# A chunked RWKV-7 scan with one transition matrix per chunk, made before the scan

## The reference

```
def step(state, inp):
    r_t, w_t, k_t, v_t, kk_t, a_t = inp
    sa = einsum('bhvk,bhk->bhv', state, -kk_t)
    state = (state * w_t[:, :, None, :] + sa[..., None] * (kk_t * a_t)[:, :, None, :]
             + v_t[..., None] * k_t[:, :, None, :])
    return state, einsum('bhvk,bhk->bhv', state, r_t)
```

## Time and profile before

| what | value |
|---|---|
| median of 3 runs | 2389.5 us (2381.62 to 2393.41) |
| the profiled execution, its own time | 2394.83 us |
| its span | 2392.7 us |
| TensorE busy | 2250.3 us, 94% |
| VectorE, ScalarE, GpSimd busy | 52%, 39%, 31% |
| TensorE's granted clock, mean | 0.977 |

### The profile page before, as it was taken

One profiled execution on the slowest core, in us unless ns is written; L12 is line 12 of the kernel. 1 busy time (PEld: TensorE's weight loads), 2 busy tenths in 40 slices (PEclk: granted clock), 3 DMA queues, 4 the chain that ended last, 5 costly groups with the idle time before them and its releaser, 6 DMA issues.

```text
span 2392.7 us, 46390 instructions
## 1 busy us (share of the span) xinstructions
PE 2250.3 (94%) x19640; PEld 1712.6 (72%) x19640; DVE 1246.5 (52%) x2035; ACT 943.4 (39%) x1681; POOL 735.8 (31%) x384
## 2 busy tenths in 40 slices
PE   8999989999979998988888889999998999999998
PEld 6885778888867647777777777777887666754476
DVE  5028254023155666767777534794213999736123
ACT  4238444233234433444444443554323222343133
POOL 2310334444414203111111033444431433430246
PEclk9999999999979998999999999999997999999999
DMA  4312123233212210000000122343231333222232
GB/s 143 111 60 78 62 72 96 88 101 93 88 42 80 88 44 9 10 10 10 10 10 10 39 71 79 117 179 124 82 106 71 106 117 114 89 87 78 71 94 82
DMA packets 49882, 180.64 MB, mean 75 GB/s; under 512 B 5600, under 2 KB 5856, under 8 KB 49440
## 3 DMA queue, kind: packets, MB, share of 16 engines
q1 hardware_dynamic: 46064, 166.82, 21.6%
q10 hardware_dynamic: 3632, 11.08, 1.2%
HBM read 167.33 MB, written 10.55 MB: 74 GB/s over the span
## 4 chain that ended last, share of the span: by engine, by line
PE 72%; issue 12%; DVE 5%; ACT 5%; POOL 4%; DMA 0%; POOLq 0%; ACTq 0%; DVEq 0%; SPq 0%
PE ps L603 15%; PE ps L604 15%; PE ps L605 15%; PE ps L606 6%; POOL ring_lo L2266 4%; PE ps L904 2%; PE ps L865 2%; PE ps L651 2%; PE ps L895 1%; PE ps L1101 1%; PE ps L722 1%; PE ps L737 1%; PE ps L712 1%; PE ps L1122 1%; PE ps L813 1%
## 5 line engine op out<-in xcount | busy, mean ns | idle before, releaser
L2266 POOL TENSOR_TENSOR ring_lo<-ring,ring_hi 128x1024 fp32r<-128x1024 f32 x240 | 589.8, 2465 | 1019.1 <-ACT ring_hi L1158 1019.0
L605 PE MATMUL ps<-u_lo,ring_hi 128*128 128x512 f32 x968 | 384.8, 398 | 0.0
L1158 ACT ACTIVATE ring_hi<-ring 128x1024 fp32r<-128x1024 f32 x240 | 251.4, 1052 | 105.4 <-DMA ring<-in_wall 102.0
L603 PE MATMUL ps<-mlp_u_hi,ring_hi 128*128 128x512 f32 x512 | 204.6, 400 | 13.6 <-DVE u_lo L1744 9.0
L606 PE MATMUL ps<-arena,ring 128*128 128x512 f32 x480 | 210.5, 594 | 6.0 <-ACT arena L1627 3.3
L605 PEld LDWEIGHTS ps<-u_lo,ring_hi 128*128 128x128 f32 x968 | 183.9, 190 | 43.5
L603 PE MATMUL ps<-mid_hi,ring_hi 128*128 128x512 f32 x512 | 203.3, 397 | 2.6 <-POOL ring_lo L2266 2.6
L604 PE MATMUL ps<-mlp_u_hi,ring_lo 128*128 128x512 f32 x512 | 203.2, 397 | 0.0
L605 PE MATMUL ps<-mid_lo,ring_hi 128*128 128x512 f32 x512 | 202.5, 396 | 0.0
L604 PE MATMUL ps<-mid_hi,ring_lo 128*128 128x512 f32 x512 | 202.5, 395 | 0.0
L603 PE MATMUL ps<-in_u_hi,ring_hi 128*128 128x512 f32 x480 | 193.8, 404 | 5.8 <-POOL gs_lo L2354 2.8
(11 more groups left out here) (434 smaller groups left out, 4335.6 us busy)
## 6 DMA issues: line engine op xcount, KB each, us to landing
ring<-in_wall SPq DMA_DIRECT2D x273, 512.0 KB, 3.7
s_tables<-arena ACTq DMA_DIRECT2D x16, 512.0 KB, 2.7
arena<-s_tables SPq DMA_DIRECT2D x16, 512.0 KB, 3.7
arena<-bias_lines SPq DMA_DIRECT2D x16, 448.0 KB, 4.3
arena<-in_lora SPq DMA_DIRECT2D x8, 384.0 KB, 3.0
h<-in_x SPq DMA_DIRECT2D x1, 2048.0 KB, 8.0
out<-arena ACTq DMA_DIRECT2D x8, 256.0 KB, 2.9
consts<-in_consts SPq DMA_DIRECT2D x1, 1152.0 KB, 14.1
```

The costliest lines, as they stand in the source:

```text
L603: nc.tensor.matmul(y, w_hi, high, start=x == 0, stop=False)
L605: return nc.tensor.matmul(y, w_hi, low, start=False, stop=x == k - 1)
L1158: nc.scalar.activation(ring_hi[:, slot], ring[:, slot], ACT.Copy).then_inc(sem("weights_high"), 1)
L2266: G.tensor_tensor(ring_lo[:, slot], ring[:, slot], ring_hi[:, slot].bitcast(F32), ALU.subtract).then_inc(sem("weights_split"), 1)
```

## The change

The scan of states is written in another form. With `Q = T alT` and the part of `u` that does not depend on the state, `T (Ma v)`, both made for all chunks at once, the state after a chunk is `decay * (step S + added)`, with one 64 x 64 matrix `step = 1 + Q (ka, be)` per chunk. So the values `u` need no round trip in a step.

- New on TensorE: `al` turned (`each_turned_al`, with the turned values, which move here from level 5); `Ma v` in the last level (`last_inner`); `T` times both for all chunks (32 products with 128 columns); `Q` times `ka`, `be` (24) and `Q` times `M0`, `M1` (28). Gone are `w`, `u`, and the two additions to it per step. The previous pair's variances move from the start to behind level 1. The gate product of the next pair moves out of the scan, as two whole products at level 5. The bonus quarters use two corners of the array each.
- VectorE: only one scaling of each state from PSUM in a step (`S`), with one or two larger operations behind each. The features' operations are spread behind single updates of the levels, the subtraction of the decay sums goes, and `al` is made from `ro` moved by one token.
- ScalarE: no work in the steps but few features; one table set for logarithm and exponential; `decays` of direction 1 move from level 4 to the scan. GpSimd: two copies of half tiles, and features direction by direction.
- SyncE: blocks 2 and 3 of the product `o` are loaded after the last pair's scan.

Matmuls in the eight pairs: 5800 before, 6448 after.

```diff
+            def each_turned_al(d, F, v=None):
+                for c in range(NCH):
+                    for e in range(2):
+                        rows, crossed, at = ...
+                        if v is not None:
+                            mm = nc.tensor.matmul(O[0][rows, at], v[rows, at], const("center", 0, CH)[rows, :], start=True, stop=True)
...
+                        mm = nc.tensor.matmul(A[d][crossed, at], F["al"][rows, at], const("eye", 0, CH)[rows, :], start=True, stop=True)
...
                 if prev:
-                    out_variances(prev)
+                    pe.wait_ge(sem("o_copied"), prev(2, 1))
+                each_turned_al(0, F[0], pair_tile(vTr, n))
+                each_turned_al(1, F[1])
...
+                    if nxt and l == LEVELS - 1:
+                        pe.wait_ge(sem("turned"), n(4, 2))
+                        hidden_product(nxt, 2, 0, 3)
...
+                        if prev and l == 1 and d == 1:
+                            pe.wait_ge(sem("v_turned"), n(1, 1))
+                            out_variances(prev)
...
-                for j in range(NCH):
...
+                for d in range(2):
+                    pe.wait_ge(sem("t_updated"), n(10, 2 * (LEVELS - 2) + d + 1))
+                    pe.wait_ge(sem("inner_taken"), n(6, 3 + d))
+                    for j in range(NCH):
...
+                            mm = nc.tensor.matmul(ps[crossed, 4 * d * SEQ + c * 2 * CH:4 * d * SEQ + (c + 1) * 2 * CH],
+                                                  R[d]["T"][crossed, at], joined[d][crossed, :, at], start=True, stop=True)
+                    mm.then_inc(sem("inner_ready"), 1)
...
+                            mm = nc.tensor.matmul(C[d][rows, at], R[d]["Q"][crossed, at], F[d][("ka", "be")[e]][crossed, at],
+                                                  start=True, stop=True)
...
+                            mm = nc.tensor.matmul(A[d][rows, at], R[d]["Q"][crossed, at], R[d][("M0", "M1")[e]][crossed, at],
+                                                  start=True, stop=True)
...
+                for j in range(1, NCH):
...
+                        pe.wait_ge(sem("state_ready"), n(14, 2 * (j - 1) + d + 1))
...
+                        state_added(j, d, False)
...
+                            mm = nc.tensor.matmul(B[d][rows, at], R[d]["step"][rows, at], R[d]["S"][rows, at], start=False, stop=True)
+                        mm.then_inc(sem("s_ready_rw"), 1)
...
+                        if j > 1:
+                            outputs(j - 1, d)
+                    if j < 5:
+                        bonus_quarter((j - 1) // 2, 2 * ((j - 1) % 2))
+                        bonus_quarter((j - 1) // 2, 2 * ((j - 1) % 2) + 1)
...
+                        TS(R[d]["S"][:, to * CH:(to + 1) * CH], bank(4 * d + 1)[:, c * CH:(c + 1) * CH],
+                           p_end[parity][d][:, c:c + 1], None, ALU.mult).then_inc(sem("state_ready"), 1)
...
+                        nc.scalar.preload_act_table_set("natural_log_exp_and_others")
```

More of the change, by code:

```diff
@@ new lines, in of_step, with state_added @@
+                def of_step(j, d):
+                    c = j if d == 0 else NCH - 1 - j
+                    return c, slice(c * CH, (c + 1) * CH)
+                def state_added(j, d, alone):
+                    _, at = of_step(j, d)
+                    for e in range(2):
+                        mm = nc.tensor.matmul(B[d][e * HEAD:(e + 1) * HEAD, at], F[d][("ka", "be")[e]][:, at], v_u[d][e][:, at],
+                                              start=True, stop=alone)
+                    return mm
@@ new lines, in outputs @@
+                def outputs(j, d):
+                    _, at = of_step(j, d)
+                    for e in range(2):
+                        rows = slice(e * HEAD, (e + 1) * HEAD)
+                        if j:
+                            nc.tensor.matmul(O[d][rows, at], R[d]["S"][rows, at], F[d]["ro"][rows, at], start=True, stop=False)
+                    for e in range(2):
+                        rows = slice(e * HEAD, (e + 1) * HEAD)
+                        mm = nc.tensor.matmul(O[d][rows, at], v_u[d][e][:, at], R[d][("M0", "M1")[e]][:, at],
+                                              start=j == 0, stop=True)
+                    return mm
@@ L1001, in pair @@
+                for d in range(2):
+                    if d == 0:
+                        pe.wait_ge(sem("inner_taken"), n(6, 5))
+                    else:
+                        pe.wait_ge(sem("inner_added"), n(6, 1))
+                    pe.wait_ge(sem("turned"), n(4, 2 * d + 2))
+                    for j in range(1, NCH - 1):
+                        _, at = of_step(j, d)
                         for e in range(2):
                             rows, crossed = slice(e * HEAD, (e + 1) * HEAD), slice((1 - e) * HEAD, (2 - e) * HEAD)
[L1003 to L1008, removed]
@@ L2131, in _ @@
-            first, last = (lambda per, c=0: c), (lambda per, c=0: (DT - 1) * per + c)
-            for step in range(6):
-                features(first, feats[0], p_end[0], step)
-            over_pairs(pair)
-            out_scaled(last, feats[(DT - 1) % 2])
-            out_gated(last, feats[(DT - 1) % 2])
+                        if (l, d) == (1, 0):
+                            bonus_terms(n, F, 0)
+                        if nxt and (l, d) == (1, 1):
+                            decay_sums(nxt, G, 0)
@@ L2137, in _ @@
+            final = feats[(DT - 1) % 2]
+            for d in range(2):
+                out_scaled(last, d)
+            for d in range(2):
+                out_with_bonus(last, final, d)
+            for d in range(2):
+                out_gated(last, final, d)
+            out_summed(last)
             y_low(last)
@@ L2326, in _ @@
             features(first, feats[0], 1)
-            pool.wait_ge(y_taken, FIRST_TILE["o"])
-            stage_v(first)
             for d in range(2):
```

455 lines of the change are left out of this document (231 added, 224 removed).

## The result

| | before | after |
|---|---|---|
| median of 4 runs, us | 2391.45 (2381.62 to 2393.68) | 2421.61 (2418.16 to 2428.61) |
| profiled execution, span, us | 2392.7 | 2421.1 |
| TensorE's granted clock, mean | 0.977 | 0.979 |

The ratio is 1.0138, 95% interval 1.0101 to 1.0175: slower by 30 us. Forecast were 2373 and a range of 2352 to 2393, so the time lies outside it, on the other side of no change.

A forecast was written before the change was run, and what follows sets the result against it. TensorE, busy 94%, was taken as the bound. Levels +2.45 and scan -3.8 gave -1.35 us a pair, -10.8 for eight; first pair -2.0, last -1.4, decayed state -2.4: -16.6, so 2373 us, range 2352 to 2393.

The forecast's parts named there:

- Steps of the scan: Scan from first outputs on: groups of two products at 0.165 us, 1.32 a step without bonus pieces, 11.2 in all.
- Preparation: Scan before its first outputs: wide products 3.5 us, 24 products 1.4, wait for `Q` 0.3, last products 1.9; 8.1 in all.
- VectorE in the steps: Scan steps: VectorE's work is shorter in sum than TensorE's and decides only from step 5 on, within the last 1.75 us.
- Levels: Levels of a pair: longer by 2.45 us, from variances, waits for masks and a gate product, less turned values and a stop.
- The stop before the last halves goes: Level 5: idle time for "issue" and ScalarE disappears as exponentials move away; -1.0 us a pair, -0.3 if "issue" stays.
- The two new waits for VectorE's masks: Levels: first feature product waits for masked `Ma`, +0.5 us; second stack of level 4 waits for masks, +0.9 a pair.
- Start: Start of a pair: no change, since the variances leave but turning `al` and the values takes the same time.
- Supply: Rival, start and level 5: instructions come too slowly for four-corner products; about 2 us lost a pair, 2389; chance 0.21.
- VectorE's transposes behind GpSimd: Rival, levels 3 and 4: transposes wait for GpSimd operations, +1.1 us a pair, 2382; chance 0.12.
- The clock in every scan: Rival: waits in each scan lower TensorE's granted clock, costing 30 us in all, 2403; chance 0.10.
- More gain: Rival, scan: 128-column products cost 0.07 us each and group changes nothing; 2 us a pair more won, 2357; chance 0.15.
- The -2.4 for VectorE's decayed state: Scan of the trace's second pair: the slow decayed-state operation goes and the new scaling reads PSUM, saving 2.4 us.

The follow-up runs named there:

- e1: Changed kernel with all TensorE products of a scan step regrouped by array shape, the same products; 2389.13 us, ratio 0.9990 to the kernel before.
- e5: Kernel before, with the 64 small four-corner score products at the start of each pair issued twice; 2418.59 us, ratio 1.0109.
- e2: Changed kernel with only the outputs regrouped: state parts of both directions, then values' parts of both; 2409.67 us, ratio 1.0080.
- e3: Changed kernel with outputs reordered so no product stands right behind the one it adds to, as many shape changes; 2426.97 us, ratio 1.0154.

## Why the prediction was wrong, point by point

*Steps of the scan, the step that failed.* The prediction put "about 0.05 is lost at each change of group" and "in groups of two at 0.165, so 1.32 a step". The first outputs and steps were to take 11.2 us; they took 15.25. What was read as a loss for any change of group in the earlier trace rows is none between groups of one shape, which follow at 0.12, and 0.14 to 0.15 where the shape changes. The trace of the kernel before had this already. Between the two lines of the earlier trace rows at 962.49 and 963.11, which the prediction averaged over, stand three more groups of one shape:

```profile
962.66 0.29 PE L1048 MATMUL ps<-arena,sq 128*64 128x64 f32 x4
962.77 0.29 PE L1044 MATMUL ps<-sq,ring_hi_values 128*64 128x64 f32 x4
962.89 0.29 PE L1048 MATMUL ps<-arena,sq 128*64 128x64 f32 x4
```

The groups start 0.17, 0.11, 0.12 and 0.22 us after each other: four times 0.12 and 0.14 for one change. The kernel before has its changes between larger groups, where an average hides them; the new order, direction by direction, makes eight in a step. The rate of a mixed stretch was taken over to another mixture.

With the shapes sorted (e1) the same products take 10.4 us and the scan 19.36, where 19.3 was forecast. That they meet is luck: the steps are 0.8 shorter than their forecast of 11.2, since e1 has fewer changes than the forecast had counted a loss for, and the preparation is 0.8 longer.

*Preparation.* Forecast 8.1, measured 8.9 (1001.2 to the first outputs at 1010.1). The 32 products of 128 columns were put at 3.5 and took 3.2; the 24 products and the wait for the copy of `Q` were put at 1.7 and took 2.15, of it 0.47 for the wait; the last part, 32 products put at 1.9, took 2.45, with three changes of shape between the additions and the products behind them, and one more in front of the first outputs: four times 0.145 is 0.58, and the miss in this part is 0.55.

*VectorE in the steps.* It was to decide only from step 5 on. It hardly decides anywhere: VectorE stood idle 33.2 us in all for TensorE's L1099, TensorE 1.4 us for its scalings, in eight waits.

*Levels.* Forecast +2.45, measured +3.29. The variances are there as new work, 1.9 us (from 1035.62 on, 0.97 and the next 0.95), and the table-load wait of 1.35 stays, as said. Three terms failed. "The stop before the last halves goes" was put at -1.0; ScalarE's part of it went, but the stops for issue grew, to 1.58 in the rows above and moved into the dense products, by 0.66 a pair over all levels. The two new waits for VectorE's masks, put at +0.5 and +0.9, were 0.10 and 0.17 a pair. And what TensorE works on in the levels grew by some 3.5 us where 2.05 was put; about 0.3 of it is the slow clock of one pair, and the rest is not taken apart here.

*Start.* Forecast 0, measured +0.37 in the changed kernel and +0.63 in e1, with the new stop of some 1 us in the 48 turned products; without it the start would be the shorter for the change.

*Rivals.* Supply was put at 2 us a pair. By the rows its stops grew by 1.55 a pair, and e5 gave 0.053 a product for the 0.055 that the rival was built on. The stops are there and grow with dense products, as it said, though as stops between blocks and not as a rate. It was the smaller part of the error, since the scan alone missed by 4.8 us a pair, and as a rival without the other cause it ended at 2389. The Trainium skill (Runtime: NRT & Kernel Launch, "Instruction fetch mechanics") calls the fetch mostly hidden; these runs show 2 to 4 us of stops a pair where small products are dense. The prediction took that rule to give the stops another cause. The count of 256 instructions from stop to stop fits the blocks of which that section of the Trainium skill speaks, and points to the fetch; "mostly hidden" does not hold here. That the fetch itself is what TensorE waits for is not seen in any view. VectorE's transposes behind GpSimd: all 64 of line 2152 took 711 to 714 ns, those too that ran wholly beside a GpSimd operation; wrong. The gate operation of level 5 (L2112), which was to wait for GpSimd, took 743 to 847 ns. The clock in every scan: one scan of seven, with 0.57 from 1252 to 1260 and 25.91 us instead of 24.18; the other six took 24.18. The kernel before had one such scan too, so this explains nothing of the difference. More gain: wrong in the changed kernel, and its "changes of group nothing" was nearer the truth for groups of one shape.

*The range.* No case had the scan itself slower. Every rival took the forecast's TensorE rate as given, because TensorE's rate was the one thing read straight from rows; it was read as an average over a stretch in which shapes seldom alternate.

*What stays open.* The changed kernel's first pair and its last scan are not taken apart, nor is the added work in the levels. The -2.4 for VectorE's decayed state held: the scan of that pair, 25.55 before and 2.4 over its neighbours, takes 24.18 after, like theirs.

## What to carry to other kernels

Write down the array shape (rows by columns) of each small product and count where it changes in the order on TensorE: here each change costs 0.14 to 0.15 us, as much as two small products, so sort products by shape within a step before products are traded for shorter chains. A rate read from a stretch holds for that stretch's order of shapes; take the price of a group and the price of a change apart, from two places with different shares of them. And where corners run four at a time, look whether TensorE's stops for "issue" stand 256 instructions apart, and spread the long products among the dense ones: moving two 1 us products a pair won 5.4 and 5.8 us here, though shorter stops are shown for 2.0 us of the first and for 0.4 of the second.

## What was not expected of the hardware

- A change between 128-row and 64-row products: 0.142 us from 34 changes (e1) and 0.146 from 14 (e2), whatever the products depend on (e3). From results of 64 columns to results of 128 in the same 64\*64 corners (L1099 to L952, 1011.13 to 1011.30) there is none, 0.17 us for a group of two.
- An f32 product of 64 rows with 128 columns takes 0.10 us in two corners (32 in 3.2), one with 64 columns 0.06.
- 347 of 348 stops for "issue" stand at every 256th of TensorE's instructions, weight loads and waits counted, the same place in twelve traces; two neighbouring ones are 3.3 to 4.3 us apart in 173 cases of 174.
- 64 more four-corner products in a stretch that was already dense cost 3.4 us: 0.030 each, as in a short run, and one such stop.
